# One unrolled pipeline of 128 query tiles for four attentions, in place of four looped ones, and its inputs prepared in the stages ahead

## The reference

```python
h = rms_norm(x, norm_mix_g)
proj = h @ w_in        # q, k, v of four mixers, indexer columns, 4 * 1024 gate columns
o_swa = sliding_window_attention(...)   # 4 heads of 64, window 128, T5 bias, sinks
o_fox = forgetting_attention(...)       # 4 heads, causal, forget-gate bias
o_sb  = stick_breaking_attention(...)   # 4 heads, strictly causal, no softmax
o_dsa = dsa_attention(...)              # 4 heads, top 256 keys by an indexer, T5 bias
merged = sum(sigmoid(gate_b) * (o_b @ w_branch[b]) for the four)
x = x + merged @ w_out
x = x + hierarchical_moe(rms_norm(x, norm_ffn_g))
```

## Time and profile before

| | us |
|---|---|
| median of three runs | 1957.18 (1955.75 to 1960.36) |
| the profiled execution | 1958.25 |
| its span, first to last instruction | 1956.6 |
| TensorE busy | 1727.9 (88% of the span) |
| VectorE busy | 1327.5 (68%) |
| ScalarE busy | 827.2 (42%) |
| GpSimd busy | 409.6 (21%) |

### The profile page before, as it was taken

One profiled execution on the slowest core, in us unless ns is written; L12 is line 12 of the kernel. 1 busy time (PEld: TensorE's weight loads), 2 busy tenths in 40 slices (PEclk: granted clock), 3 DMA queues, 4 the chain that ended last, 5 costly groups with the idle time before them and its releaser, 6 DMA issues. The chain is left out here.

```text
span 1956.6 us, 26588 instructions
## 1 busy us (share of the span) xinstructions
PE 1727.9 (88%) x8546; PEld 1428.4 (73%) x8546; DVE 1327.5 (68%) x1813; ACT 827.2 (42%) x970; POOL 409.6 (21%) x299
## 2 busy tenths in 40 slices
PE   6799989999999959888867989813999999999996
PEld 5677768788888848767766867713888888888774
DVE  4256893799990025685555973262999999998895
ACT  5255311211212126444542121121777777777673
POOL 1111230222222200000001200033433333334442
PEclk8899999999999979898877989966999999999998
DMA  4523331333222147362658523236999999999992
GB/s 151 161 97 129 129 140 44 122 110 108 91 103 90 72 98 150 64 132 52 137 124 321 218 95 118 96 141 258 386 383 385 380 376 361 364 379 373 375 378 107
DMA packets 146147, 381.59 MB, mean 195 GB/s; under 512 B 53935, under 2 KB 55983, under 8 KB 145948
## 3 DMA queue, kind: packets, MB, share of 16 engines
q1 hardware_dynamic: 128260, 353.18, 53.0%
q0 software_dynamic: 17824, 27.58, 3.9%
HBM read 338.79 MB, written 68.63 MB: 208 GB/s over the span
## 5 line engine op out<-in xcount | busy, mean ns | idle before, releaser
L1626 DVE TENSOR_TENSOR ex_wl<-ex_raw,ex_wh 128x2048 fp32r<-128x2048 f32 x192 | 437.3, 2286 | 39.2 <-ACT ex_wh L1622 38.9
L1622 ACT ACTIVATE ex_wh<-ex_raw 128x2048 fp32r<-128x2048 f32 x192 | 367.7, 1918 | 141.1 <-PE ex_upp L2132 53.8
L75 PE MATMUL sg_gp<-hT_hi,gs_wh 128*128 128x512 f32 x512 | 200.4, 391 | 3.2 <-PEq L64 3.2
L77 PE MATMUL sg_gp<-hT_hi,gs_wl 128*128 128x512 f32 x512 | 199.9, 390 | 0.0
L76 PE MATMUL sg_gp<-hT_lo,gs_wh 128*128 128x512 f32 x512 | 199.8, 390 | 0.0
L761 ACT ACTIVATE gs_wh<-gs_raw 128x1024 fp32r<-128x1024 f32 x30 | 31.8, 1061 | 263.1 <-PE sg_gp L77 263.1
L1239 PE MATMUL at_ops<-at_v,at_pT 128*128 128x65 f32 (+1 forms) x984 | 127.8, 274 | 0.0
L1239 PEld LDWEIGHTS at_ops<-at_v,at_pT 128*128 128x128 f32 x984 | 123.9, 197 | 1.1
L716 POOL TENSOR_TENSOR gs_wl<-gs_raw,gs_wh 128x1024 fp32r<-128x1024 f32 x30 | 72.1, 2403 | 241.3 <-ACT gs_wh L761 241.3
L75 PEld LDWEIGHTS sg_gp<-hT_hi,gs_wh 128*128 128x128 f32 x512 | 96.5, 189 | 24.1 <-issue 4.2
L576 PE MATMUL pj_ps<-hT_hi,gs_wh 128*128 128x512 f32 x272 | 112.1, 412 | 0.0
(11 more groups left out here) (286 smaller groups left out, 3928.8 us busy)
## 6 DMA issues: line engine op xcount, KB each, us to landing
ex_raw<-in_w_expert_up SPq DMA_DIRECT2D x128, 1024.0 KB
ex_raw<-in_w_expert_down SPq DMA_DIRECT2D x64, 1024.0 KB, 21.1
gs_raw<-in_w_gate SPq DMA_DIRECT2D x32, 512.0 KB
gatesT<-sg_go SPq DMA_DIRECT2D x32, 512.0 KB
mg_g<-gatesT SPq DMA_DIRECT2D x8, 2048.0 KB
gs_raw<-in_w_qk SPq DMA_DIRECT2D x17, 512.0 KB
qkh<-pj_oh SPq DMA_DIRECT2D x17, 512.0 KB, 2.6
qkl<-pj_ol SPq DMA_DIRECT2D x17, 512.0 KB, 3.9
```

The costliest lines, as they stand in the source:

```text
L75: pe.matmul(out, a_hi, b_hi, start=(k == 0), stop=False)
L77: last = pe.matmul(out, a_lo, b_hi, start=False, stop=(k == len(lhs) - 1))
L1622: act.activation(ring.wh[r][:, :, :], ring.raw[slot][:, :, :], ACT.Copy).then_inc(ring.w_high, 1)
L1626: dve.tensor_tensor(ring.wl[r][:, :, :], ring.raw[slot][:, :, :], ring.wh[r][:, :, :].bitcast(F32), ALU.subtract).then_inc(ring.w_low, 1)
```

## The change

In `project`: the indexer units begin one chunk later (`FIRST_UNIT_CHUNK` 5); the high parts of the four V pieces are made two at a time in the last chunks (`pieces_at`), where two of them stood behind the last chunk; three small scalings of `gc` stand behind the loop over x tiles where they stood inside it; `vtok` has 65 columns for each of 11 V heads, the last of them one.

In `select_and_gate`: the T5 tiles stay in SBUF (`slots.t5`, the dsa ones with the far bias already taken off); POOL makes the masks and zeroes the padding of two of the four head slots; SP loads heads 0 and 1 between two gate stores.

In `attention`: no setup block and no mixers. One block, no loops, units 0 to 127 in one pipeline (16 heads, in the order fox, sb, dsa, swa), with the same order of PE within a step. A ring of four head slots: SP loads head H+4 when head H's scores are done. V is one tile for all heads, loaded by kind. The two switches of ScalarE's function table stand between units. Swa's shape step waits for the transposes of unit u-2, where it waited for their weights.

```diff
-FIRST_UNIT_CHUNK = 4
+FIRST_UNIT_CHUNK = 5
...
+            for p in range(QK_CHUNKS):
+                low(p)
+            pool.wait_ge(added, len(UNITS))
+            pool.wait_ge(x_turned, NT)
+            for s in range(3):
+                pool.memset(with_one(xt[s], HALF)[:, :, HD:HD + 1], 1.0).then_inc(ones_set, 1)
+            for p in range(QK_CHUNKS, pieces):
                 low(p)
...
+            def pieces_at(ck):
+
+
+                if ck < QK_CHUNKS - 2:
+                    return [ck + 1]
+                n = QK_CHUNKS - 1 + 2 * (ck - QK_CHUNKS + 2)
+                return range(n, min(n + 2, QK_CHUNKS + 4))
...
-                if ck >= 2 and ck + 1 < QK_CHUNKS + 4:
-                    high(ck + 1)
+                if ck >= 2:
+                    for p in pieces_at(ck):
+                        high(p)
...
-                if t == 2:
-                    dve.wait_ge(gain_loaded, 16)
-                    for n, q in enumerate((SWA_Q, FOX_Q, DSA_Q)):
-                        dve.tensor_scalar(gc[:, q:q + 2], gc[:, q:q + 2], SCALE, None, ALU.mult).then_inc(gain_done, 1)
             h_lo(NT - 1)
+            dve.wait_ge(gain_loaded, 16)
+            for q in (SWA_Q, FOX_Q, DSA_Q):
+                dve.tensor_scalar(gc[:, q:q + 2], gc[:, q:q + 2], SCALE, None, ALU.mult).then_inc(gain_done, 1)
...
+                if k == NG - 6:
+                    sp.wait_ge(slots.zeroed, 4)
+                    sp.wait_ge(c_stored, 96)
+                    for H in range(2):
+                        load_head(sp, slots, H, qkh, qkl, crow)
...
+            pool.wait_ge(w_low, GATE_PIECE + 9)
+            slots.zero(pool, (0, 1))
+            pool.wait_ge(slots.zeroed, 4)
+            low(9)
+            low(10)
...
+            load_v(KINDS[0])
+            sp.wait_ge(slots.zeroed, 8)
+            load_head(sp, slots, 2, qkh, qkl, crow)
+            load_head(sp, slots, 3, qkh, qkl, crow)
+            load_v(KINDS[1])
+            for H in range(len(HEADS)):
+                kind, h = HEADS[H]
+                if H + 4 < len(HEADS):
+                    after(sp, logits, (H + 1) * NT - 1)
+                    load_head(sp, slots, H + 4, qkh, qkl, crow)
+                if H == 2:
+                    load_v(KINDS[2])
+                    load_v(KINDS[3])
+                after(sp, finished, (H + 1) * NT - 1)
...
+            for u in range(N + 2):
+                if 1 <= u <= N and kind_of(u - 1) != "sb":
+                    weigh(u - 1)
+                if 0 < u < N and table(kind_of(u)) != table(kind_of(u - 1)):
+                    act.preload_act_table_set(table(kind_of(u)))
+                if u < N and kind_of(u) == "sb":
+                    soften(u)
+                if u >= 2:
+                    copy_turned(u - 2)
...
-            with pe.Fori(0, 2) as it:
-                score(it, 0)
-                for u in range(N + 2):
-                    if u + 1 < N:
-                        score(it, u + 1)
-                    if 1 <= u <= N:
-                        turn(it, u - 1)
-                    if u >= 2:
-                        apply(it, u - 2)
+            pe.wait_ge(slots.masks_done, 6)
+            score(0)
+            for u in range(N + 2):
+                if u + 1 < N:
+                    score(u + 1)
+                if 1 <= u <= N:
+                    turn(u - 1)
+                if u >= 2:
+                    apply(u - 2)
```

More of the change, by code:

```diff
@@ L976, in q_row, with wait @@
+    def wait(self, engine):
+        engine.wait_ge(self.sem, self.n)
+KINDS = ("fox", "sb", "dsa", "swa")
+HEADS = [(kind, h) for kind in KINDS for h in range(NH)]
+ATT_UNITS = [(H, i) for H in range(len(HEADS)) for i in range(NT)]
+PER_KIND = NH * NT
+SLOTS_QK = 4
 def q_row(kind):
@@ L986, in kv_head, with v_head, __init__, add @@
     return {"dsa": 0, "swa": h // 2}.get(kind, h)
-def mixer(nc, kind, next_kind, m, ident, selm, sel_at, load, qk_loaded, v_loaded, otok):
-    units = [(i, s) for s in range(2) for i in range(NT)]
-    N = len(units)
-    keys = near_blocks if kind == "swa" else all_blocks
+def v_head(kind, h):
+    return {"fox": 0, "sb": 4, "swa": 8, "dsa": 10}[kind] + kv_head(kind, h)
+class HeadSlots:
+    def __init__(self, nc, c, sem):
+        sb = lambda n, s, d=F32: c.enter_context(nc.sbuf_tensor(n, s, d, side="right"))
+        self.parts = {n: [] for n in ("q", "kh", "kl", "qc")}
+        self.t5 = sb("at_t5", [P, 2 * NH, BAND])
+        self.far = sb("at_far", [P, NH])
+        self.sink = sb("at_sink", [P, NH])
+        self.sink_neg = sb("at_sink_neg", [P, NH])
+        self.identb = sb("at_identb", [P, P], BF16)
+        self.causal = sb("at_causal", [P, P], BF16)
+        self.strict = sb("at_strict", [P, P], BF16)
+        self.loaded = [sem(f"at_qk_loaded{s}") for s in range(SLOTS_QK)]
+        self.masks_done = sem("at_masks_done")
+        self.zeroed = sem("at_zeroed")
+        self.add(nc, c, (0, 1))
+    def add(self, nc, c, numbers):
+        for s in numbers:
+            for n, made in self.parts.items():
+                made.append(c.enter_context(nc.sbuf_tensor(f"at_{n}{s}", [P, T], FR, side="right")))
+        self.q, self.kh, self.kl, self.qc = (self.parts[n] for n in ("q", "kh", "kl", "qc"))
+    def zero(self, engine, numbers):
+        for s in numbers:
+            for t in (self.qc, self.kl):
+                engine.memset(t[s][HD:P, :].bitcast(F32), 0.0).then_inc(self.zeroed, 1)
@@ L1095, in _ @@
         @block.vector
         def _(dve):
-            dve.sem_inc(shaped, 2)
-            dve.sem_inc(scanned, 2)
-            dve.sem_inc(finished, 2)
-            dve.sem_inc(stored[0], 16)
-            dve.sem_inc(stored[1], 16)
-            def steps_of(u):
-                i = units[u][0]
-                return {"fox": 1, "sb": 0, "swa": 3 if i == 0 else 2 if i == 1 else 1,
-                        "dsa": 2 if i == 0 else 1 if i == 1 else 3}[kind]
-            per = sum(steps_of(u) for u in range(N))
@@ L1166, in finish @@
-            def finish(it, u):
-                i, s = units[u]
-                O = m["o_ps"][u % 2]
-                dve.wait_ge(summed, it * N + u + 1 + 2)
-                if i == 0:
-                    dve.wait_ge(stored[s], it * 16 + 16)
+                chain.did(dve.tensor_tensor(X[:, n0:W], S[:, n0:W], T5, ALU.add))
+                chain.did(bias_and_peak(X[:, 0:n0], S[:, 0:n0], sel[:, 0:n0], -PICKED, part[u % 2][:, :]))
+                chain.wait(dve)
+                bias_and_peak(X[:, n0:W], X[:, n0:W], sel[:, n0:W], part[u % 2][:, 0:1], peak).then_inc(done, 1)
@@ L1174, in finish @@
                     return
[L1175 to L1188 removed]
+                total = den[u % 4][:, :] if kind == "swa" else O[:, HD:HD + 1]
@@ L1217, in score, with turn @@
                                          start=(j == 0 and not masked), stop=(j == 1), skip_group_check=masked)
-                last.then_inc(logits, 1)
-            def turn(it, u):
-                pe.wait_ge(shaped if kind == "sb" else weighed, it * N + u + 1 + 2)
-                first = BAND - len(keys(units[u][0])) * P if kind == "swa" else 0
+                last.then_inc(logits[u // PER_KIND], 1)
+            def turn(u):
+                after(pe, shaped if kind_of(u) == "sb" else weighed, u)
+                first = BAND - len(keys(u)) * P if kind_of(u) == "swa" else 0
```

495 lines of the change are left out of this document (226 added, 269 removed).

## The result

The changed kernel takes 1879.62 us (median of 4 runs, 1877.28 to 1879.87) beside 1956.95 for the kernel before on the same chip: a ratio of 0.960, 95% interval [0.958, 0.962]. The profiled execution took 1879.8 us with a span of 1878.2, 78.4 less than before; the sum of the prediction was 73.8. TensorE is busy 1707.1 us (91% of the span).

A forecast was written before the change was run, and what follows sets the result against it. TensorE sets the pace, but idles about 100 us in projection and attention, with slow clock behind gaps. Gains 1.2 + 13.0 + 5.0 + 13.3 + 41.3 = 73.8 take the span from 1956.6 to 1882.8; forecast 1884, range 1868 to 1904.

The forecast's parts named there:

- what the last V load stands behind: Projection's end: last V piece loaded only after chunk 15's store, issued at 258.1, landing at 262, leaving a 3.5 us gap.
- that a table load is always paid for: Attention, between kinds: ScalarE's table load takes 1.28 us and no barrier hides it now.
- a wait at the V tiles of 2 to 5 us: Sign in the changed profile: TensorE waits 2 to 5 us at the first V tile on POOL's low part.
- one of 1.5 to 4 us for fox's V: Sign in attention: the first application, or the matmul in its place, waits 1.5 to 4 us for V.
- Gains moved: First x tiles: VectorE no longer waits for gain columns between tiles; 1.2 us gained, bounds 0 and 2.2.
- Indexer: Projection: units one chunk later remove 11.0 us of gap and 2.0 of slow clock; 13.0 gained, bounds 10 and 13.6.
- V weights: Projection's end: splitting them earlier cuts TensorE's 8.6 us wait to some 3.5; 5.0 gained, bounds 2 and 10.4.
- Preparation beside the gates: Gate stage: 16 head loads and four memsets fit into idle time of SP and POOL; cost 0.
- Start of attention: Between gates and first score: 15.9 us gained, less 2.6 waiting for fox's V; net 13.3, bounds 10 and 15.9.
- Heads in the full pipeline: Attention: drained heads plus 1.1, 0.7, 0.5, 0.4 us give fox 17.0, sb 20.5, dsa 17.7, swa 7.2.
- Kind changes: Attention: table load and large units running against small ones cost 1.3 us at each of three changes of kind.
- rival 2: More gained: kinds overlap well and the V gap closes, 5.4 us more in projection, up to 8.7 in attention; 1870, chance 0.14.

The follow-up runs named there:

- the run with the copy first: The changed kernel, but ScalarE makes the high part of chunk 15's output ahead of the V piece it waits for: 1878.39 us, ratio 0.958.

## Why the prediction was right, and where it was off

The time came as said (1879.6 for 1884), and so did where the gains lie. That the sum is off by only 4.6 us (78.4 for 73.8) is in part luck: attention gave 8.7 more than forecast (the wait for V counted in it), and the V weights 3.6 and the gains 1.0 less. Three steps were wrong: what the last V load stands behind, what a dsa head costs without its increments, and that a table load is always paid for. Two of the signs named for the profile failed with them, a wait at the V tiles of 2 to 5 us (6.2) and one of 1.5 to 4 us for fox's V (0.8).

- **Gains moved**: 1.2 predicted. The first chunk starts at 24.37 instead of 24.60, so 0.2, which is within the spread (23.97 to 24.89 in kernels that are alike there). The wait for the columns was slack of the chain that follows, as far as these rows tell.
- **Indexer**: 13.0. Right: with the gains 13.8 by the end of the chunks, and 13.3 given back when it is undone, 0.5 of that by a later start of the first chunk (24.89 for 24.37).
- **V weights**: 5.0 predicted, 1.4 came (15.3 at the start of the gates less 13.8), outside the bounds. From the issue of the last load to the first V tile the prediction had 7.9 us (258.1 to 266) and 8.6 came (246.65 to 255.21): nearly as reckoned. The step that failed is the start of it: "SP issues that load at 258.1", 4.8 ahead of the chunks' end (262.9), was carried over, and now it stands only 2.4 ahead (246.65 for 249.02). So the wait is 6.2 and not 3.5, and from the first V tile to the end of the V tiles it takes 68.9 us, 0.9 longer than before. Of the 2.4 us the change itself makes about 2, by the rows of the run with the copy first: the V pieces split earlier bring POOL's low part in front of VectorE's, which then waits 1.4 to 2.0 us, and the store and the load wait behind that. No run takes GpSimd's operation out of the way alone. The reason that I gave for the lower bound, VectorE's lost chunk, is not it: with that chunk back the issue is 2.7 ahead and the wait 5.9. The run with the last V load ahead of the stores takes the load out of this chain, and all of the 6.2 goes.
- **Preparation beside the gates**: 0, right; the stage's 32 chunks take what they took.
- **Start of attention**: gap 15.9, right to 0.1. V is waited for 0.8 us, not 2.6: issued at 687.2 and wanted about 4.5 us later, it had landed by 692.5, after 5.2. The measurement lies under both rows that the prediction went by (5.6 and 8.2). The fit that the prediction quotes from the Trainium skill ("DMA: Bandwidth & Descriptors", Anatomy of one DMA) stands there for transfers that GpSimd issues, and V is issued by SP; its estimate, 4.4 us and a wait of 0.3, is 0.8 and 0.5 below what was measured. The first head, predicted 25.0 with that wait, took 24.4.
- **Heads in the full pipeline**: fox 17.1 (17.0), sb 20.2 to 20.5 (20.5), swa 7.1 (7.2). The small amounts added to drained heads were right. Dsa 16.6 (17.7): the term took the increments that VectorE carries as free. The change leaves them out (lines 1154 and 1163 before), and putting two back costs 3.6 us over the four heads, most of the 4.2 that were missed.
- **Kind changes**: 3 x 1.3 predicted, 0.6 came, in the last fox head. The step "no barrier hides it now" failed where sb ends: VectorE does. One of the three boundaries has no table load at all.

By where the 47.4 us of attention came from: drains about 13 (16.4 less the slow stretch); increments 4; the ring and early loads with the blocks gone, the rest, some 30. In swa the two 18.5 to 18.9 us heads became 9.3 without any change of the draining, 18.9 us; at the two other kind changes 5.9 and about 6 (7.1 less the increments). How this rest divides between blocks, loads and the clock behind the gaps was not measured one by one; that loops as such are nothing much was. The clock's part can be bounded. Behind the first head the kernel before has five stretches at half clock, 48 us together, two of them in these windows:

```profile
797.00:804.00 7.00, 6.66 (x28) 5.31 (x28) 5.08 (x9) 3.34 (x9) 0.00 (x0) 0.51 0.00 0
...
972.00:982.00 10.00, 9.63 (x45) 9.02 (x45) 5.52 (x26) 5.80 (x21) 0.00 (x0) 0.53 0.01 2
```

TensorE is busy 32 us in the five, and after none of them is left. Work at half clock takes up to twice as long, so by an estimate from these rows they cost up to 16 us; it is an upper bound, since part of that work waits for other engines anyway.

No head's load is waited for inside attention, no "issue" gap recurs, and no rival was needed: rival 2, kinds overlap well, is the nearest, with its attention half come true (8.7 us more than forecast) and its V half not.

## What to carry to other kernels

Where an engine waits for the last of a row of prepared pieces, look at what the transfer of that piece is queued behind, not at how early the arithmetic on it was put: issuing one load ahead of two stores gave 7 to 10 us, all that was done to the arithmetic on the pieces 1.4. An operation that is moved on GpSimd can hold up VectorE, and with it a store and the load behind that. When pipelines are joined, price a full-pipeline head as a drained one plus the foreign work mixed in, but first take out what exists only for the loop (semaphore increments that carry no data, between operations that depend on each other), and price a fixed cost at a boundary by which engine waits there. A shorter gap is worth less than its length while the clock falls all the same: here 10.7 us of gap were worth 7.5, since the slow stretch then lay in the work behind the gap.

## What was not expected of the hardware

- Half the clock came in two kernels inside attention, in the last sb head, with only waits of 1.3 and 1.4 us ahead of it: for 10 us in the kernel drained every 16 units, and for 7 us ahead of the wait where dsa begins in the unrolled kernel before. The same waits in other sb heads, and in this head of the kernel before, brought no such stretch. Its cause is open.
- The slow stretch at the start of attention spans gap and work together. Behind 4.9 idle us it covers 10 us from the first score on; with 15.7 idle us it lies mostly in the gap, and the first head is 3 us shorter.
- VectorE and GpSimd block each other for a whole operation of 128x1024: 1.21 us where VectorE is first or alone, 2.59 and 3.23 behind GpSimd's 2.4 us one.
- An increment of a semaphore by itself takes VectorE 0.15 us between dependent operations, in each of the 24 units where one stands there.
